# Seven-product quads of a feed-forward stage: four products joined to 512 columns, two weight copies and two VectorE operations moved

## The reference, cut to what matters

```python
def swiglu(h, w_gate_up, w_down):          # h: 512 x 1024, D_FF = 2816
    gate, up = jnp.split(h @ w_gate_up, 2, axis=-1)
    return (jax.nn.silu(gate) * up) @ w_down
```

## Time and profile before

| | before |
|---|---|
| median of 3 runs | 1292.29 us |
| profiled execution, its own time | 1292.28 us |
| its span | 1290.5 us |
| PE busy | 1282.9 us |
| DVE busy | 918.5 us |
| ACT busy | 555.2 us |
| mean granted TensorE clock | 0.999 |

### The profile page before, as it was taken

The page is one execution under the profiler, slowest core; times in us unless marked ns, Lnnn a source line. Parts: engine busy times, 40 slices in busy tenths (PEclk is TensorE's granted clock), DMA queues, the critical chain, the costliest instruction groups (busy, mean ns, idle before and its releaser), DMA issues.

```text
span 1290.5 us, 19358 instructions
## 1 busy us (share of the span) xinstructions
PE 1282.9 (99%) x7292; PEld 1100.6 (85%) x7292; DVE 918.5 (71%) x1413; ACT 555.2 (43%) x1162; POOL 254.8 (20%) x290
## 2 busy tenths in 40 slices
PE   9999999999999999999999999999999999999998
PEld 7888778888888998899988878888888998899986
DVE  7988856346689994289955778557789983489942
ACT  6347455124533660066622347425433660167612
POOL 0222154212322002100021226423221002000020
PEclk9999999999999999999999999999999999999999
DMA  7333222232433423333323341133333323343232
GB/s 249 101 96 115 91 72 93 83 98 82 130 90 95 126 83 99 98 115 105 106 86 113 107 118 57 50 98 98 99 98 98 115 92 99 96 124 99 83 98 98
DMA packets 96843, 130.69 MB, mean 101 GB/s; under 512 B 5328, under 2 KB 62160, under 8 KB 96752
## 3 DMA queue, kind: packets, MB, share of 16 engines
q1 hardware_dynamic: 94976, 127.29, 31.7%
q10 hardware_dynamic: 1776, 2.18, 0.6%
HBM read 124.67 MB, written 2.10 MB: 98 GB/s over the span
## 4 chain that ended last, share of the span: by engine, by line
PE 98%; DVE 0%; DMA 0%; ACT 0%; SPq 0%; issue 0%; ACTq 0%; POOL 0%; DVEq 0%; POOLq 0%
PE ps L815 18%; PE ps L819 18%; PE ps L818 18%; PE ps L995 6%; PE ps L997 6%; PE ps L996 6%; PE ps L983 5%; PE ps L984 2%; PE ps L1478 1%; PE ps L1474 1%; PE ps L1477 1%; PE ps L1307 1%; PE ps L1323 1%; PE ps L1336 1%; PE ps L1196 1%; PE ps L1227 1%
## 5 line engine op out<-in xcount | busy, mean ns | idle before, releaser
L737 POOL TENSOR_SCALAR w_hi<-raw 128x1024 fp32r<-128x1024 f32 x156 | 182.0, 1168 | 935.8 <-PE ps L997 359.3
L1506 DVE TENSOR_TENSOR w_lo<-raw,w_hi 128x1024 fp32r<-128x1024 f32 x161 | 203.0, 1265 | 180.1 <-POOL w_hi L737 177.2
L815 PE MATMUL ps<-f_hi,w_hi 128*128 128x512 f32 x720 | 281.2, 391 | 0.2 <-DVEq L1902 0.2
L819 PE MATMUL ps<-f_hi,w_lo 128*128 128x512 f32 x720 | 280.3, 389 | 0.0
L818 PE MATMUL ps<-f_lo,w_hi 128*128 128x512 f32 x720 | 280.2, 389 | 0.0
L995 PE MATMUL ps<-zq_r,quad_hi 128*128 128x256 f32 x640 | 181.4, 283 | 0.0
L996 PE MATMUL ps<-zq_r,quad_hi 128*128 128x256 f32 x640 | 181.1, 283 | 0.0
L815 PEld LDWEIGHTS ps<-f_hi,w_hi 128*128 128x128 f32 x720 | 135.2, 188 | 28.8 <-DVEq L1902 0.4
L819 PEld LDWEIGHTS ps<-f_hi,w_lo 128*128 128x128 f32 x720 | 135.2, 188 | 28.3
L818 PEld LDWEIGHTS ps<-f_lo,w_hi 128*128 128x128 f32 x720 | 135.2, 188 | 27.8
L995 PEld LDWEIGHTS ps<-zq_r,quad_hi 128*128 128x128 f32 x640 | 121.4, 190 | 3.9 <-ACT copied L2754 1.2
(11 more groups left out here) (276 smaller groups left out, 2274.3 us busy)
## 6 DMA issues: line engine op xcount, KB each, us to landing
quad_raw<-in_w_gate_up SPq DMA_DIRECT2D x64, 512.0 KB
raw<-in_w_down SPq DMA_DIRECT2D x44, 512.0 KB
raw<-in_w_gate_up SPq DMA_DIRECT2D x48, 256.0 KB
raw<-in_w_out SPq DMA_DIRECT2D x20, 512.0 KB
raw<-in_w_in SPq DMA_DIRECT2D x19, 512.0 KB
raw<-in_xa_wkv SPq DMA_DIRECT2D x16, 512.0 KB
raw<-in_w_in SPq DMA_DIRECT2D x17, 256.0 KB
raw<-in_xa_wq SPq DMA_DIRECT2D x8, 512.0 KB
```

The lines of the kernel that those rows point to most:

```text
L737: pool.tensor_scalar(w_hi[:, slot], raw[:, slot], 1.0, 1.0, ALU.mult, ALU.mult).then_inc(s_hi, 1)
L815: ins = pe.matmul(o, whi, rhi, start=start, stop=False)
L819: return pe.matmul(o, wlo, rhi, start=False, stop=stop)
L1506: dve.tensor_tensor(w_lo[:, slot], raw[:, slot], w_hi[:, slot].bitcast(F32), ALU.subtract).then_inc(s_lo, 1)
```

## The change

- Products 3 and 7 are joined as 2 and 4 are (`APART`), so that their activations lie side by side and their high x high parts land in the right halves of banks 2 and 1.
- In every product all steps with high weights come first, and then the four with low weights; PE waits for the high weights before the first and for the low weights before the second.
- The third copy (u3) takes the whole bank instead of half of it.
- A new VectorE operation, `second_tile_apart`, adds the right halves of banks 2 and 3 to the second tile. `s_c` counts three per quad instead of two.
- On VectorE, `first_tile(n - 1)` moves behind low weights 1 and 3, and `f_low(n, 1)` from the end of an odd quad into the next one, behind its first `weight_sum`.
- On ScalarE, the high weights 3 of n + 1 and 1 of n + 2 are made behind the third copy of quad n; they were made at the start of the next quad, between the copy of the apart halves and the SiLU.

```diff
-APART = (2, 4)
+APART = (2, 4, 3, 7)
...
-            def quad_ready(l, q, i):
+            def quad_high_ready(l, q, i):
 
                 if q == QUAD0[l, 0]:
                     pe.wait_ge(s_zql, 7 * l + Z_LOWS.index(i) + 1)
+                pe.wait_ge(s_wh, HIGH[q, i])
+
+            def quad_low_weights(q, i, o):
+
                 pe.wait_ge(s_wl, LOW[q, i])
+                lo, hi = z_rows(i)
+                for k in range(4):
+                    ins = pe.matmul(o, kind_lo(q, i)[:, k, :], zq_r[:, hi, :][:, k, :], start=False, stop=k == 3,
+                                    skip_group_check=True)
+                ins.then_inc(s_p, 1)
 
             def quad_product_apart(l, q, i, both, o):
 
-                quad_ready(l, q, i)
+                quad_high_ready(l, q, i)
                 for k in range(4):
                     pe.matmul(both, kind_hi(i)[:, k, :], low_and_high(i, k), start=False, stop=False, skip_group_check=True)
-                    ins = pe.matmul(o, kind_lo(q, i)[:, k, :], low_and_high(i, k)[:, 1, :], start=False, stop=k == 3,
-                                    skip_group_check=True)
-                ins.then_inc(s_p, 1)
+                quad_low_weights(q, i, o)
...
-                        quad_product(l, q, 3, d, False)
+                        quad_product_apart(l, q, 3, d_wide, d)
                         pe.wait_ge(s_cp, COPIED[q, "u2"])
-                        quad_product(l, q, 7, a, False)
+                        quad_product_apart(l, q, 7, a_wide, a)
                         first_product(n + 1)
...
+                    def second_tile_apart(n):
+
+                        ff = ff_u if n % 2 else ff_g
+                        dve.wait_ge(s_c, 3 * (QUAD0[l, c] + n) + 1)
+                        dve.tensor_tensor(halves(ff[:, 1, :]), halves(ff[:, 1, :]), bank_pair(qg, n, 2, 1),
+                                          ALU.add).then_inc(s_c, 1)
+
...
                         if more:
                             weight_sum(q + 1, 1)
-                        if n:
-                            first_tile(n - 1)
+                        if n and not up:
+                            f_low(n - 1, 1)
                         if n == 0:
                             rest()
                         if more:
                             weight_low(q + 1, 1)
                         if n:
                             weight_low(q, 3)
+                            first_tile(n - 1)
                             free(n - 1)
...
                         second_tile(n)
+                        second_tile_apart(n)
                         if n == 0:
                             later()
                         if up:
                             gated(n, 1)
-                            f_low(n, 1)
+                    f_low(n_quads - 1, 1)
...
-                        act.activation(home(qg, n, 3), home(qg, n, 1), ACT.Copy).then_inc(s_cp, 1)
+                        act.activation(ps[:, bank(qg + n, 3), :], ps[:, bank(qg + n, 1), :], ACT.Copy).then_inc(s_cp, 1)
...
                         if n:
                             copy_apart(n - 1)
-                            weight_high(c, n, 3)
-                        if more:
-                            weight_high(c, n + 1, 1)
+                        elif more:
+                            weight_high(c, 1, 1)
                         if up:
-                            act.wait_ge(s_c, 2 * q)
+                            act.wait_ge(s_c, 3 * q)
                             act.activation(ff_g[:, 0, :], ff_g[:, 0, :], ACT.Silu).then_inc(s_q_silu, 1)
                         copy_fifth(n)
...
                         copy_third_sum(n)
+                        if more:
+                            weight_high(c, n + 1, 3)
+                        if n + 2 < n_quads:
+                            weight_high(c, n + 2, 1)
                         if not up:
-                            act.wait_ge(s_c, 2 * q + 1)
+                            act.wait_ge(s_c, 3 * q + 2)
                             act.activation(ff_g[:, 1, :], ff_g[:, 1, :], ACT.Silu).then_inc(s_q_silu, 1)
```

More of the change, by code:

```diff
@@ L971, in zf @@
                 return zf_hi[:, k, :], zf_lo[:, k, :]
-            def quad_ready(l, q, i):
+            def quad_high_ready(l, q, i):
                 if q == QUAD0[l, 0]:
                     pe.wait_ge(s_zql, 7 * l + Z_LOWS.index(i) + 1)
+                pe.wait_ge(s_wh, HIGH[q, i])
+            def quad_low_weights(q, i, o):
                 pe.wait_ge(s_wl, LOW[q, i])
+                lo, hi = z_rows(i)
[3 more added lines that the diff above has]
+                ins.then_inc(s_p, 1)
             def quad_product_apart(l, q, i, both, o):
-                quad_ready(l, q, i)
+                quad_high_ready(l, q, i)
                 for k in range(4):
                     pe.matmul(both, kind_hi(i)[:, k, :], low_and_high(i, k), start=False, stop=False, skip_group_check=True)
-                    ins = pe.matmul(o, kind_lo(q, i)[:, k, :], low_and_high(i, k)[:, 1, :], start=False, stop=k == 3,
-                                    skip_group_check=True)
-                ins.then_inc(s_p, 1)
+                quad_low_weights(q, i, o)
             def quad_product(l, q, i, o, start):
-                quad_ready(l, q, i)
+                quad_high_ready(l, q, i)
+                lo, hi = z_rows(i)
                 for k in range(4):
[L992 to L998, removed]
+                    pe.matmul(o, kind_hi(i)[:, k, :], zq_r[:, hi, :][:, k, :], start=start and k == 0, stop=False,
+                              skip_group_check=True)
+                    pe.matmul(o, kind_hi(i)[:, k, :], zq_r[:, lo, :][:, k, :], start=False, stop=False, skip_group_check=True)
+                quad_low_weights(q, i, o)
             def quads(l, c):
@@ L1012, in quads @@
                     b, a, d = home(g0, n, 0), home(g0, n, 1), home(g0, n, 2)
-                    b_wide, a_wide = ps[:, bank(g0 + n, 0), :], ps[:, bank(g0 + n, 1), :]
+                    b_wide, a_wide, d_wide = (ps[:, bank(g0 + n, i), :] for i in (0, 1, 2))
                     quad_product(l, q, 5, d, True)
@@ L2166, in free @@
                     def free(n):
-                        dve.wait_ge(s_c, 2 * (QUAD0[l, c] + n) + 2)
+                        dve.wait_ge(s_c, 3 * (QUAD0[l, c] + n) + 3)
                         dve.nop().then_inc(s_free[(qg + n) % 2], 4)
@@ L2183, in second_tile @@
                         dve.tensor_tensor(halves(ff[:, 1, :]), bank_pair(qg, n, 2), copied[:], ALU.add).then_inc(s_c, 1)
+                    def second_tile_apart(n):
[3 more added lines that the diff above has]
+                                          ALU.add).then_inc(s_c, 1)
                     def gated(n, p):
                         q = QUAD0[l, c] + n
-                        dve.wait_ge(s_c, 2 * q + 2 - p)
+                        dve.wait_ge(s_c, 3 * q + 3 - p)
                         dve.wait_ge(s_q_silu, 2 * (q // 2) + 2 - p)
@@ L2747, in copy_fifth @@
                         if q:
-                            act.wait_ge(s_c, 2 * q - 1)
+                            act.wait_ge(s_c, 3 * q - 2)
                         act.activation(copied[:, 1, :], home(qg, n, 2), ACT.Copy).then_inc(s_cp, 1)
```

## The result

The changed kernel takes 1311.28 us (median of 4 runs, 1311.15 to 1311.57), the kernel before 1292.26 us (1292.11 to 1292.39, 4 runs, the first three being those above): a ratio of 1.0146, 95% interval 1.0134 to 1.0158. That is 19.0 us slower; 1308 was predicted. The span of the profiled execution grew from 1290.5 to 1309.6 us, so by 19.1, and all of it lies in the four runs of quads. From the first step of a run to the first step of the down product behind it, the runs took 60.30, 100.42, 60.30 and 100.41 us and now take 64.28, 105.97, 64.34 and 105.96: 4.0 + 5.55 + 4.0 + 5.55 = 19.1 us.

What follows compares the result with a forecast made beforehand. TensorE bounds the kernel before; after the change a VectorE-ScalarE-TensorE loop of 21.25 us per two quads would. Losses of 12.5, 3.2 and 0.2 us, together 15.9, on 1292.29 gave 1308 us; forecast 1300 to 1312, range 1298 to 1315.

Steps and rivals of the forecast that it cites:

- Joined steps: Products 3 and 7 on TensorE: 0.03 us less per joined product, 64 times, 1.9 us less in all.
- The loop: VectorE's second tile to first_tile, ScalarE's SiLU and copy u2, product 7, third copy, back: 21.25 us for two quads.
- Second tile 0.72 behind which the add waits: On VectorE, second_tile takes 0.72 us instead of 0.60 because the new add waits for its result.
- first_tile behind low weights 1 and 3: this is the part that costs.: In odd quads ScalarE's SiLU waits for the later first_tile; from that SiLU to copy u2 2.87 us pass.
- High weights moved: On ScalarE, 1.04 us between apart copy and SiLU go; no cost, help only if first_tile is ready.
- The sum over pairs: Sixteen pairs of quads: ten lose 12.5 us, four last ones 3.2, first pairs of 10-quad runs 0.2; together 15.9 us.
- A: Rival: not slower; ScalarE's regained 1.04 us carry the late first_tile, only joined steps count, 1290.4 us; chance 0.11.
- B: Rival: only copy c1, wanted before product 2, is late; u2 is covered; about 1297 us; chance 0.09.
- C: Rival: hand-offs not shown in the trace lengthen the loop to 21.7 us or more; 1314 us and up; chance 0.11.

Runs made afterwards that it cites:

- e12: The ScalarE and VectorE orders of e11, but products 3 and 7 not joined, no new add, narrow third copy; 1290.34 us, ratio 0.9983.
- e11: Changed kernel with ScalarE's copies u2, c1, c5 and high weight 7 made earlier, VectorE's free and gated(n-1, 0) later; 1288.20 us, ratio 0.9967.
- e8: Changed kernel with only first_tile put back ahead of low weights 1 and 3; 1301.53 us, ratio 1.0070.
- e2: Changed kernel with first_tile, f_low(n, 1) and high weights 3 and 1 back in their old places; 1311.48 us, ratio 1.0148.
- e3: The moves and step order without the join: products 3 and 7 plain, no new add, narrow third copy; 1293.68 us, ratio 1.0009.
- e4: Changed kernel without the new VectorE add second_tile_apart, so its result is incomplete; 1293.39 us, ratio 1.0006.
- e6: Changed kernel with ScalarE's copies zero and c1 ahead of the SiLU of the even quad's second half; 1309.10 us, ratio 1.0129.

## Why the prediction was right, and where it was off

**Joined steps, 1.9 us less.** Right in kind and size (1.40 against 1.43 us; e12 to e11 2.1 us). The bars would have said forty.

**The loop sets the pace, not TensorE.** Right: 21.51 us a pair where 21.25 were counted; waits before products 2 and 7 of the odd quads of middle pairs, and none in even ones; VectorE waiting for high weight 7. Off in size: c1 cost 0.77 us, not 0.55; VectorE's wait for high weight 7 is 0.55 by its bracket and 0.64 by the starts (593.23 + 0.60 to 594.47), not 0.9, since the hand-off next named takes part of that time. The main term that was too small is the hand-off behind first_tile: 0.72 was counted, and it is 0.93 with free alone behind it (592.30 to 593.23), 0.89 with free and gated (582.25 to 583.14); in the even quad this 0.17 lies in the loop. The second is product 7: its joined steps take 1.48 us behind the wait (596.33 to 597.81), 0.07 more than the 1.41 counted. With a few hundredths at other places, some of them the other way, that makes 0.26 us a pair, 2.6 us in ten, and most of the 3.3 us between 1308 and 1311.3.

**Second tile 0.72 behind which the add waits.** Right: 577.18 to 577.90 to 578.63. The Trainium skill ("VectorE: DVE Perf Modes", section "The DRAIN you can't avoid") says, from eight copies with a semaphore after each, that the semaphore costs nothing extra. The changed kernel disagrees, as the rows before did, where the next operation waits for that semaphore: 0.60 us without a wait, 0.72 with one, 0.9 with a semaphore-only instruction between.

**"first_tile behind low weights 1 and 3: this is the part that costs."** Half right. In the changed kernel its late place does cost 9.8 of the 19 us (e8, 1301.5 against 1311.3). But undoing all three moves brings nothing (e2, 1311.5), and the moves without the join lose at most 0.2% (e3), so it can't be called the cause of the loss by itself. What turned the balance is the added operation (e4): it stands twice in the loop, and takes its whole length out of TensorE's time once the slack is gone. The prediction counted that operation, but named another part as the one that costs.

**High weights moved: no cost, and a help "only if first_tile is ready".** That condition is what e8 and e2 show. With first_tile early, the kernel with the high weights and f_low moved takes 1301.5 us and the one with both in their old places 1311.5: together these two moves save 10.0 us. In the changed kernel, with first_tile late, ScalarE idles before that SiLU instead (1.31 us at 593.02), as the prediction said; what the two moves bring there was not run. In e2, whose loop is as long as the changed kernel's, the part from the odd second tile to the even one is 11.87 us instead of 11.39, and the one from the even to the odd 9.76 instead of 10.14. The share of each of the two moves is open; neither was run alone.

**The sum over pairs.** Ten at 1.25, four at 0.8, two at 0.1 gave 15.9; measured 19.1. Three loop pairs of a 10-quad run are 4.5 of its 5.55 us, so first and last together are 1.0 where 0.9 was counted. The classes of pairs and their small terms were nearly right; the main error is the 0.26 us in each loop pair.

**Rivals.** A (not slower) fell at the rows it named: first_tile starts 3.26 us into the odd quad (589.04 to 592.30), with 1.7 allowed. B (only c1 late) fell, product 7 waits 0.74 us for u2. C (more is lost) was the nearest: a hand-off that the trace of before did not show made the loop longer, by 0.26 us a pair where C assumed 0.45.

## What to carry to other kernels

Where three in-order queues hand work round in a cycle, add up the cycle and compare it with the bound engine's own time; the busy share of the near-full engine (91%) does not show it, and single waits don't add up: removing the one for c1 gave back 2.2 of 19 us and moved the rest to the next consumers of the same queue (e6). Before adding an operation to such an engine, first take the operations that nobody waits for out of the way of those that TensorE waits for. And price a matmul by the distance of two starts, never by its bar.

## What the runs showed of the hardware that was not expected

A semaphore-only instruction that waits for VectorE's last operation, placed right behind it, delays the next one to 0.9 us from the start of the first, against 0.72 where the next operation waits itself and 0.60 without a wait; with an independent operation in between, the cost was gone (e11: first_tile at 577.24, the weight sum at 577.84, gated at 578.44).

A wait cost TensorE a little more than its delay. The four joined steps right behind one took 1.01 to 1.03 us (596.33 to 597.34, 591.25 to 592.28), against 0.93 where nothing was waited for (583.40 to 584.33); why is open.
